# A decoder layer with a 32-expert mixture: the first expert's rows turned from an early gather and one-hot products, and the gathers and loads reordered around them

## Chip, cores and metric

One core of one Trainium2 chip. The metric is the device time of one launch in microseconds (us), the median over runs. The granted TensorE clock stands in the profile as a share of full speed: 1.00 is 2.4 GHz, 0.50 is 1.2 GHz.

## The reference, cut to what matters

```python
x  = x + merged @ w_out                      # (1024, 1024), the "x2" of the kernel
h2 = rms_norm(x, norm2_g)
# hier_moe: top-1 of 4 groups, then top-2 of its 8 SwiGLU experts
gl = h2 @ w_gr + b_gr;  g_idx = argmax(gl);  p_g = softmax(gl)[g_idx]
el_sel = (h2 @ w_er + b_er).reshape(N, 4, 8)[g_idx]
top_v, top_i = top_k(el_sel, 2)
w = softmax(top_v) * p_g
out[token] += w * (silu(xb @ w_gate[e]) * (xb @ w_up[e])) @ w_down[e]    # 32 experts, blocks of 128 rows
```

All of it in float32. The 1024 tokens are eight tiles of 128, and each expert serves its tokens in one block of up to 128 rows.

## The kernel before, in words

The kernel is written engine by engine, with semaphores; each engine runs its own list in order. float32 products are made of three products of split operands (high times high, high times low, low times high; `split3`, L105 to L107), so every weight piece is copied to a rounded "high" by ScalarE (`w_high`, L1186) and its remainder "low" is subtracted by VectorE (`w_low`, L1747).

**Output projection and routing.** `out_proj(cnt, ...)` runs 16 units, eight tiles for each half of the columns; VectorE adds the residual (`add_residual`, L1673) into `x2`. In the second eight units the router follows each tile: TensorE turns half a tile (`turn_half`, L838), ScalarE copies it out (`turned_half`, L1168), TensorE makes 36 logits (`route_half`, L851), VectorE finds group and experts (`top_group`, `two_experts`), TensorE counts earlier tokens of each expert (`positions_of`, L862 and L864), VectorE makes one-hot rows of the slot (`place_rows`, L1738 to L1741), and `rows_of` (L871) accumulates a table of token numbers: after eight tiles column e of `ids_rows` holds expert e's tokens. SyncE stores each finished tile of `x2` to `x2_dram` and to the output.

**Experts.** One round for each expert. POOL gathers its rows from `x2_dram` with an indirect DMA (`gather_rows`) into `xe[j % 4]`, TensorE turns them (`turn_x`, L571; for the first expert L956), ScalarE scales them by the norm's gain (`xs`, L1194) and makes `xeH`, VectorE makes `xeL`, and TensorE runs gate and up (`gate_up`, four pieces) and down (`down`, two pieces of the expert before). The result is added to rows gathered again from the output and scattered back (POOL).

**Weight loads.** Each expert has six pieces of 1 MB. SyncE issues all 192 in order of use (`load_piece(q)`) into ten slots; from q = 10 on each waits until the piece ten before it has been used (`w_used`). Pieces 0 to 3 are the first expert's gate and up, 4 to 7 the second's, 8 and 9 the first's down pieces. Pieces 0 and 1 are issued after the first eight projection units, 2 after the fourth store of `x2`, 3 after the last projection unit. Pieces 4 and later wait for the first gather (`xe_landed0`), and 8 waits for all stores of `x2`.

## Time and profile before

| what | value |
|---|---|
| median of 3 runs (lowest, highest) | 1482.78 us (1482.42, 1483.3) |
| the profiled execution's own time | 1481.47 us |
| its span | 1479.7 us |
| busy: PE, PEld, DVE, ACT, POOL | 96%, 81%, 68%, 56%, 28% |
| loads and other traffic on q1 | 263.79 MB of 286.39 MB |

PE is TensorE's matmul side and PEld its weight load, DVE VectorE, ACT ScalarE, POOL GpSimd, SP SyncE (SPq its queue). A `[... <-X]` at the end of a timeline row is idle time before it and what ended it. "DMA share" is the mean busy share of the core's 16 DMA engines. A matmul's duration holds its latency; the distance from start to start is what it costs in a stream.

### The profile page before, as it was taken

What the parts mean: (1) busy time and instruction counts of PE and PEld (TensorE: products, weight loads), DVE (VectorE), ACT (ScalarE), POOL (GpSimd) and SP (SyncE); (2) the same over time, 40 slices, a digit from 0 to 9 for tenths busy, and PEclk for the clock granted to TensorE, in tenths of its full rate; (3) what the DMA queues carried; (4) which work ended last, traced back from release to release, by engine and by line L of the source; (5) the groups of instructions that cost most, each with busy time, mean ns of one, the idle gap of its engine ahead of it and who ended that gap; (6) DMA issues with size and microseconds to landing.
All of it is one profiled execution on the core that took longest, in us unless ns stands there. A gap on an engine that the chain in (4) does not pass through costs nothing.

```text
span 1479.7 us, 19519 instructions
## 1 busy us (share of the span) xinstructions
PE 1424.3 (96%) x7296; PEld 1199.5 (81%) x7297; DVE 1008.1 (68%) x1444; ACT 828.9 (56%) x1342; POOL 407.7 (28%) x462
## 2 busy tenths in 40 slices
PE   5899999999999999999999979999999999999996
PEld 5788888888888788888888867888888888888885
DVE  6855664664574533344332567999999999999996
ACT  5653453353353322233232227888888888888883
POOL 3225424424433400000000011233333333333331
PEclk9999999999999999999999988999999999999999
DMA  7010110210210143354330549999999999999992
GB/s 220 23 44 12 51 44 1 62 43 1 61 44 0 44 115 99 86 149 121 91 142 36 198 152 385 375 386 385 392 386 387 386 389 389 393 396 393 389 384 89
DMA packets 134032, 286.39 MB, mean 194 GB/s; under 512 B 18864, under 2 KB 97840, under 8 KB 109360
## 3 DMA queue, kind: packets, MB, share of 16 engines
q1 hardware_dynamic: 119216, 263.79, 49.3%
q0 software_dynamic: 13248, 21.00, 3.8%
q8 instruction: 60, 0.98, 0.3%
q10 hardware_dynamic: 1472, 0.32, 0.1%
q14 instruction: 36, 0.29, 0.1%
HBM read 287.16 MB, written 25.17 MB: 211 GB/s over the span
## 4 chain that ended last, share of the span: by engine, by line
PE 85%; DMA 4%; DVE 4%; ACT 2%; POOL 2%; issue 2%; POOLq 0%; DVEq 0%; ACTq 0%
PE proj L105 17%; PE proj L107 16%; PE proj L106 16%; PE scores L105 6%; PE scores L107 6%; PE scores L106 6%; DMA w_slot<-in_w_up 4%; PE outs L760 2%; PE scores L693 2%; PE scores L571 1%; PE turned L105 1%; PE turned L107 1%; PE turned L106 1%; PE outs L851 1%; DVE w_low L1747 1%
## 5 line engine op out<-in xcount | busy, mean ns | idle before, releaser
L1747 DVE TENSOR_TENSOR w_low<-w_slot,w_high 128x2048 fp32r<-128x2048 f32 x192 | 430.9, 2285 | 0.1
L1186 ACT ACTIVATE w_high<-w_slot 128x2048 fp32r<-128x2048 f32 x190 | 352.6, 1907 | 20.1 <-DMA w_slot<-in_w_up 8.5
L105 PE MATMUL proj<-w_high,xeH 128*128 128x512 f32 x512 | 203.8, 398 | 3.9 <-DVE xeL L1850 1.9
L107 PE MATMUL proj<-w_high,xeL 128*128 128x512 f32 x512 | 200.6, 392 | 0.0
L106 PE MATMUL proj<-w_low,xeH 128*128 128x512 f32 x512 | 200.1, 391 | 0.0
L1376 POOL DMA_INDIRECT out<-y,ids_rows x31 | 86.5, 2791 | 342.8 <-DVE y L1860 342.8
L999 ACT ACTIVATE wCH<-wC_in 128x1024 fp32r<-128x1024 f32 x48 | 47.6, 1052 | 154.1 <-DMA wC_in<-in_w_branch_b 154.1
L1442 DVE TENSOR_TENSOR wCL<-wC_in,wCH 128x1024 fp32r<-128x1024 f32 x48 | 56.9, 1237 | 92.3 <-ACT wCH L999 92.3
L105 PEld LDWEIGHTS proj<-w_high,xeH 128*128 128x128 f32 x512 | 97.0, 189 | 25.5 <-issue 3.7
L107 PEld LDWEIGHTS proj<-w_high,xeL 128*128 128x128 f32 x512 | 96.5, 188 | 20.9
L106 PEld LDWEIGHTS proj<-w_low,xeH 128*128 128x128 f32 x512 | 96.7, 189 | 19.2
L105 PE MATMUL proj<-wBH,hTH 128*128 128x512 f32 x256 | 111.5, 435 | 0.0
L105 PE MATMUL proj<-wAH,hTH 128*128 128x384 f32 x256 | 99.1, 387 | 5.2 <-DVE wAL L1437 3.7
L107 PE MATMUL proj<-wBH,hTL 128*128 128x512 f32 x256 | 101.0, 395 | 0.0
L106 PE MATMUL proj<-wBL,hTH 128*128 128x512 f32 x256 | 100.3, 392 | 0.0
L105 PE MATMUL scores<-w_high,hidH 128*128 128x512 f32 x248 | 99.6, 402 | 0.0
L107 PE MATMUL scores<-w_high,hidL 128*128 128x512 f32 x248 | 96.9, 391 | 0.0
L106 PE MATMUL scores<-w_low,hidH 128*128 128x512 f32 x248 | 96.6, 390 | 0.0
L107 PE MATMUL proj<-wAH,hTL 128*128 128x384 f32 x256 | 87.7, 343 | 0.0
L106 PE MATMUL proj<-wAL,hTH 128*128 128x384 f32 x256 | 87.5, 342 | 0.0
L1194 ACT ACTIVATE xs<-scores,small 128x128 f32<-128x128 f32 x256 | 69.8, 385 | 5.1 <-PE scores L571 5.1
L1364 POOL DMA_INDIRECT xe<-x_rows,ids_rows x32 | 59.6, 1864 | 36.5 <-DVE ids_rows L1770 21.2
(299 smaller groups left out, 3167.4 us busy)
## 6 DMA issues: line engine op xcount, KB each, us to landing
w_slot<-in_w_gate SPq DMA_DIRECT2D x64, 1024.0 KB, 11.1
w_slot<-in_w_up SPq DMA_DIRECT2D x64, 1024.0 KB, 11.2
w_slot<-in_w_down SPq DMA_DIRECT2D x64, 1024.0 KB, 11.7
wC_in<-in_w_in SPq DMA_DIRECT2D x32, 512.0 KB, 4.8
wB_in<-in_w_in SPq DMA_DIRECT2D x16, 512.0 KB, 6.1
wA_in<-in_w_in SPq DMA_DIRECT2D x12, 512.0 KB, 5.9
x_all<-in_x SPq DMA_DIRECT2D x4, 1024.0 KB, 8.8
wC_in<-in_w_branch_a SPq DMA_DIRECT2D x16, 256.0 KB, 5.7
```

The costliest lines, as they stand in the source:

```text
L105: pe.matmul(out, lh, rh, start=start, stop=False)
L106: pe.matmul(out, lh, rl, start=False, stop=False)
L107: return pe.matmul(out, ll, rh, start=False, stop=stop)
L693: pe.matmul(SC[:, c, t0 * 128:t1 * 128], q_part[r, 0, :], k_part[r, 1 + t0:1 + t1, :].rearrange("p a b -> p (a b)"), start=q_part is qkTH ...
L760: last = pe.matmul(OB[:, 0:128], aT[:, j, :], V[:, j, :], start=(j == 0), stop=(j == i2))
L999: act.activation(wCH[sub][:, piece * 8:piece * 8 + 8, :], wC_in[sub][:, piece * 8:piece * 8 + 8, :], ACT.Copy).then_inc(S["wC_high"], 1)
L1186: act.activation(w_high[slot][:], w_in6[slot][:], ACT.Copy).then_inc(S["w_split"], 1)
L1194: act.activation(xs[:, k, :], SC[:, 0, k * 128:(k + 1) * 128], ACT.Copy, scale=g2x[:, k:k + 1]).then_inc(S["xs_done"], 1)
L1364: pool.indirect_dma_start(out=xe[j % 4][:], out_offset=None, in_=x2_dram, in_offset=ids_of(ids_rows, j), bounds_check=1023, oob_is_err=Fal ...
L1376: pool.indirect_dma_start(out=out_rows, out_offset=ids_of(ids_rows, j), in_=rows[:], in_offset=None, bounds_check=1023, oob_is_err=False). ...
L1442: dve.tensor_tensor(wCL[sub][:, r, :], wC_in[sub][:, r, :], wCH[sub][:, r, :].bitcast(F32), ALU.subtract).then_inc(S["wC_low"], 1)
L1747: dve.tensor_tensor(w_low[slot][:], w_in6[slot][:], w_high[slot][:].bitcast(F32), ALU.subtract).then_inc(S["w_lows"], 1)
```

## The change

1. Six tiles' table. `positions_of(5)` moves ahead of `route_half(14)` in unit 15, and `rows_of(4)` and `rows_of(5)` into unit 15; VectorE places tile 5 first and writes `first_ids`, the first expert's tokens of tiles 0 to 5. POOL gathers these rows into `xe[1]` at once, while tiles 6 and 7 are still being routed.
2. Tiles 6 and 7 go to the first expert by products: `x2` of each is split into `x2_high` (ScalarE) and `x2_low` (POOL), and `first_late` multiplies both with the one-hot matrix `first_pick` (VectorE) and accumulates onto the turned rows of the early gather, in two banks. The sum of squares of these rows is put together in the same way (`late_ss`, `first_r`).
3. `rows_of(6)`, `rows_of(7)` and the full table follow behind the first expert's first piece; then POOL gathers the second expert's rows first, and the first expert's (needed for the result) after them.
4. Pieces 4, 5 and 6 are loaded without a wait; piece 7, the eighth, waits until the second expert's rows have landed, and all later pieces stand behind it in SyncE's list.
5. The router's chain is two VectorE steps shorter for each tile (logits in two scaled additions of which one runs early, group mask in one). The low part of piece 2 is made in VectorE's iteration 4, and its high in ScalarE's unit 11, where both came after the units before.
6. VectorE scales the first expert's turned rows by the gain (`first_scaled`), where ScalarE did; the low part of its first half is made k by k.

```diff
-R_DIFFS, R_WEIGHTS = 90, 107
+R_DIFFS, R_WEIGHTS = 85, 102
...
+N_EARLY = 6
...
             for i in range(4, N_TILES - 1):
                 store_x2(i)
             sp.wait_ge(S["d_done"], 16)
             load_piece(3)
             store_x2(N_TILES - 1)
-            sp.wait_ge(S["xe_landed0"], DMA)
             for q in range(4, 6 * N_EXP):
+                if q == 7:
+                    sp.wait_ge(S["xe_landed1"], 2 * DMA)
                 if q == 8:
-                    sp.wait_ge(S["x2_stored"], N_TILES * DMA)
-                    sp.wait_ge(S["out_stored"], N_TILES * DMA)
+                    sp.wait_ge(S["x0_T"], 2)
+                    sp.wait_ge(S["early_stored"], 2 * N_EARLY * DMA)
+                    sp.wait_ge(S["late_stored"], 2 * (N_TILES - N_EARLY) * DMA)
                 load_piece(q)
...
+                if cnt == 15:
+                    positions_of(5)
                 if cnt >= 1:
                     route_half(cnt - 1)
...
+                if cnt == 15:
+                    rows_of(4)
+                    rows_of(5)
                 out_proj(cnt, range(5, 8))
...
+            def first_early():
+
+                pe.wait_ge(S["xe_landed1"], DMA)
+                for k in range(8):
+                    pe.matmul(first_turned(k), xe[1][:, DS(k, 128, step=8)], ident, start=(k % 4 == 0), stop=False, is_transpose=True)
+
+            def first_late(t, ks):
+
+                pe.wait_ge(S["place_step"], FIRST_HOT[t])
+                pe.wait_ge(S["x2_lows"], t - N_EARLY + 1)
+                for k in ks:
+                    for part in (x2_high, x2_low):
+                        last = pe.matmul(first_turned(k), part[t - N_EARLY][:, DS(k, 128, step=8)], first_pick[t - N_EARLY][:, :],
+                                         start=False, stop=(t == 7 and k % 4 == 3 and part is x2_low))
+                return last
+
             turn_half(15)
+            positions_of(6)
             route_half(15)
-            positions_of(6)
-            rows_of(5)
+            first_early()
+            first_late(6, range(4))
             positions_of(7)
-            rows_of(6)
-            rows_of(7)
...
+            first_late(6, range(4, 8))
+            first_late(7, range(4)).then_inc(S["x0_T"], 1)
+            first_late(7, range(4, 8)).then_inc(S["x0_T"], 1)
...
-                if cnt in (9, 10):
+                if cnt in (9, 10, 11):
                     high(w_high[cnt - 9][:], w_in6[cnt - 9][:], S[f"w_land{cnt - 9}"], DMA, S["w_split"])
...
+            for i in range(2):
+                act.activation(x2_high[i][:], x2[:, N_EARLY + i, :], ACT.Copy).then_inc(S["x2_highs"], 1)
+            act.wait_ge(S["xe_landed1"], DMA)
+            act.activation(first_sq[:], xe[1][:], ACT.Square, scale=1.0 / 32, accum_out=first_ms[:]).then_inc(S["first_sum"], 1)
+            act.wait_ge(S["xs_done"], 4)
+            for k in range(4):
+                act.activation(xeH[:, k, :], xs[:, k, :], ACT.Copy).then_inc(S["x0_H"], 1)
+            act.wait_ge(S["xs_done"], 8)
+            act.wait_ge(S["route_step"], R_DIFFS)
+            act.activation(xeH[:, 4:8, :], xs[:, 4:8, :], ACT.Copy).then_inc(S["xeH_done"], 1)
             high_piece(3)
...
+                if i == N_EARLY + 1:
+                    pool.wait_ge(S["xe_zero"], 1)
+                    pool.wait_ge(S["early_stored"], 2 * N_EARLY * DMA)
+                    pool.wait_ge(S["tables_done"], 1)
+                    pool.indirect_dma_start(out=xe[1][:], out_offset=None, in_=x2_dram[0:N_EARLY * 128, :],
...
+            for i in range(2):
+                pool.wait_ge(S["x2_highs"], i + 1)
+                pool.tensor_tensor(x2_low[i][:], x2[:, N_EARLY + i, :], x2_high[i][:].bitcast(F32), ALU.subtract).then_inc(S["x2_lows"], 1)
...
+            pool.wait_ge(S["x0_T"], 2)
+            pool.wait_ge(S["first_sum"], 1)
+            gather_rows(1)
             gather_rows(0)
-            gather_rows(1)
...
+            first_scaled(0)
+            for k in range(4):
+                dve.wait_ge(S["x0_H"], k + 1)
+                dve.tensor_tensor(xeL[:, k, :], xs[:, k, :], xeH[:, k, :].bitcast(F32), ALU.subtract).then_inc(S["x0_L"], 1)
+            dve.wait_ge(S["x0_T"], 3)
+            dve.wait_ge(S["first_sum"], 1)
+            dve.tensor_tensor(first_r[:], OB[:, 0:1], first_ms[:], ALU.add).then_inc(S["first_norm"], 1)
+            for t in range(N_EARLY, N_TILES):
+                pick_rows(t)
+            first_scaled(1)
...
+            dve.wait_ge(S["xeH_done"], 1)
+            dve.tensor_tensor(xeL[:, 4:8, :], xs[:, 4:8, :], xeH[:, 4:8, :].bitcast(F32), ALU.subtract).then_inc(S["xeL_done"], 1)
+            dve.wait_ge(S["rows_mm"], 8)
+            dve.tensor_tensor(ids_rows[:, 0:32], bank(3)[:, 32:64], w_rows[:, 0:32], ALU.add).then_inc(S["tables_done"], 1)
```

TensorE's list behind the last projection unit, before (`keyid` is the numbered token table, `xe` the gathered rows):

```order
L851 MATMUL outs<-wr,x2T 128x36 x3
L862 MATMUL scores<-mask,count_masks 128x32 [waits before_done,place_step]
L864 MATMUL scores<-before,count_masks 128x32
L871 MATMUL scores<-keyid_154,picks 128x32 [waits place_step]
L871 MATMUL scores<-keyid_154,picks 128x32
L862 MATMUL scores<-mask,count_masks 128x32 [waits before_done,place_step]
L864 MATMUL scores<-before,count_masks 128x32
```

and the same place in the changed kernel:

```order
L868 MATMUL outs<-wr,x2T 128x36 x3
L923 MATMUL turned<-consts,xe_221 128x128 [waits xe_landed1]
L923 MATMUL turned<-consts,xe_221 128x128 x3
L923 MATMUL proj<-consts,xe_221 128x128 x4
L931 MATMUL turned<-first_pick_167,x_high_231 128x128 [waits x2_lows,place_step]
L931 MATMUL turned<-first_pick_167,x_low_233 128x128
L931 MATMUL turned<-first_pick_167,x_high_231 128x128
L931 MATMUL turned<-first_pick_167,x_low_233 128x128
L931 MATMUL turned<-first_pick_167,x_high_231 128x128
L931 MATMUL turned<-first_pick_167,x_low_233 128x128
L931 MATMUL turned<-first_pick_167,x_high_231 128x128
L931 MATMUL turned<-first_pick_167,x_low_233 128x128
```

Behind these stand `positions_of(7)` and 24 more rows of L931. The turning of the gathered rows and the first eight products of tile 6 now stand ahead of the counting of tile 7.

POOL's list, before:

```order
L1351 TENSOR_TENSOR rstd_132<-ms_131,consts 128x1 [waits n2_rstd]
L1355 MEMSET xe_216 128x1024 [waits lg_done]
L1364 DMA xe_216<-x_rows,ids_rows 128x1024 [waits tables_done,x2_stored,xe_zero]
L1364 DMA xe_217<-x_rows,ids_rows 128x1024
```

and changed (`x_low` is `x2_low`; `xe_221` is `xe[1]`):

```order
L1412 DMA xe_221<-x_rows,first_ids 128x1024 [waits tables_done,early_stored,xe_zero]
L1416 TENSOR_TENSOR ms_131<-ms_131,ssq 128x1 [waits n2_sq]
L1418 TENSOR_TENSOR rstd_132<-ms_131,consts 128x1 [waits n2_rstd]
L1422 TENSOR_TENSOR late_ss<-ssq 128x1 x2
L1426 TENSOR_TENSOR x_low_233<-x_123,x_high_231 128x1024 [waits x2_highs]
L1426 TENSOR_TENSOR x_low_234<-x_123,x_high_232 128x1024 [waits x2_highs]
L1428 MEMSET xe_220 128x1024 [waits lg_done]
L1430 TENSOR_SCALAR first_r<-first_r 128x1 [waits first_norm]
L1432 TENSOR_TENSOR first_r<-first_r,consts 128x1 [waits first_norm]
L1441 DMA xe_221<-x_rows,ids_rows 128x1024 [waits x0_T,tables_done,first_sum,late_stored,xe_zero]
L1441 DMA xe_220<-x_rows,ids_rows 128x1024
```

POOL has two products of 1024 columns between the early gather and the second expert's.

SyncE's list, before:

```order
L527 DMA w_slot_190<-in_w_gate 128x2048 [waits xe_landed0]
L527 DMA w_slot_191<-in_w_up 128x2048
L527 DMA w_slot_192<-in_w_gate 128x2048
L527 DMA w_slot_193<-in_w_up 128x2048
L527 DMA w_slot_194<-in_w_down 128x2048 [waits out_stored,x2_stored]
```

and changed:

```order
L540 DMA w_slot_194<-in_w_gate 128x2048
L540 DMA w_slot_195<-in_w_up 128x2048
L540 DMA w_slot_196<-in_w_gate 128x2048
L540 DMA w_slot_197<-in_w_up 128x2048 [waits xe_landed1]
L540 DMA w_slot_198<-in_w_down 128x2048 [waits late_stored,early_stored,x0_T]
L540 DMA w_slot_199<-in_w_down 128x2048
L540 DMA w_slot_190<-in_w_gate 128x2048 [waits w_used]
```

The names' numbers differ by four between the two kernels: the first row of each is piece 4. The wait has moved from piece 4 to piece 7.

## Rows read from the trace of the kernel before

**Rows 1.** Windows: us, busy us of the engines, granted clock, DMA share, GB/s.
```profile
884.00:892.00 8.00, 2.04 (x9) 1.67 (x9) 2.37 (x2) 4.29 (x13) 3.06 (x4) 0.50 0.50 151
892.00:910.00 18.00, 17.79 (x92) 15.25 (x92) 13.09 (x21) 9.42 (x15) 0.00 (x0) 0.90 1.01 405
950.00:1000.00 50.00, 50.00 (x239) 41.96 (x238) 47.42 (x28) 42.73 (x50) 17.09 (x8) 1.00 1.00 381
1400.00:1440.00 40.00, 39.51 (x189) 32.75 (x188) 36.92 (x22) 33.41 (x36) 13.14 (x6) 1.00 1.01 385
```

**Rows 2.** The chain that ended last, expert rounds: start us, us, what.
```profile
1319.00 0.47 PE turned L571 x4
...
1336.77 0.47 PE turned L571 x4
...
1384.19 17.92 DMA w_slot<-in_w_up
...
1421.07 17.67 DMA w_slot<-in_w_up
```

**Rows 3.** Loads issued at 888.01, 889.34, 1055.67, 1375.59; us to landing at the end.
```profile
w_slot<-in_w_gate SPq DMA_DIRECT2D x1, 1024.0 KB, 7.5
...
w_slot<-in_w_up SPq DMA_DIRECT2D x1, 1024.0 KB, 13.7
...
w_slot<-in_w_down SPq DMA_DIRECT2D x1, 1024.0 KB, 6.8
...
w_slot<-in_w_down SPq DMA_DIRECT2D x1, 1024.0 KB, 18.6
```

**Rows 4.** Load issued at 844.94; us to landing.
```profile
w_slot<-in_w_gate SPq DMA_DIRECT2D x1, 1024.0 KB, 7.3
```

**Rows 5.** Timeline, a late projection unit: start us, us, what.
```profile
852.68 0.60 ACT L1168 ACTIVATE x2T<-scores 128x512 f32<-128x512 f32 x1 [0.53 <-PE scores L838]
...
854.55 0.97 PE L851 MATMUL outs<-wr,x2T 128*128 128x36 f32 x8
...
874.56 1.90 ACT L1186 ACTIVATE w_high<-w_slot 128x2048 fp32r<-128x2048 f32 x1
```

**Rows 6.** Timeline between the last projection and the first expert product.
```profile
872.62 0.69 DVE L1673 TENSOR_TENSOR x<-proj,x 128x512 f32<-128x512 f32 x1 [0.75 <-PE proj L107]
...
876.25 0.20 DVE L1706 TENSOR_TENSOR logits<-outs,logits 128x36 f32<-128x36 f32 x1 [0.62 <-PE outs L851]
...
879.23 0.22 DVE L1732 TENSOR_TENSOR keyid<-sorted,consts_late 128x64 fp32r<-128x64 f32 x1
...
882.06 0.19 DVE L1770 TENSOR_SCALAR ids_rows<-scores 128x32 int32<-128x32 f32 x1 [0.77 <-PE scores L871]
...
883.27 1.32 POOL L1364 DMA_INDIRECT xe<-x_rows,ids_rows  x1 [6.12 <-issue]
...
888.04 1.97 PE L956 MATMUL scores<-consts,xe 128*128 128x128 f32 x8 [5.88 <-DMA xe<-x_rows,ids_rows]
...
891.93 0.77 PE L105 MATMUL proj<-w_high,xeH 128*128 128x512 f32 x1 [1.92 <-DVE xeL L1850]
```

**Rows 7.** Gathers on POOL's queue issued at 883.27 and at 910 to 912; us to landing.
```profile
xe<-x_rows,ids_rows POOLq DMA_INDIRECT x1, 4.7
...
xe<-x_rows,ids_rows POOLq DMA_INDIRECT x1, 8.7
```

**Rows 8.** Groups by form, VectorE: mean ns of one.
```profile
L1741 DVE TENSOR_TENSOR picks<-consts_late,pos 128x256 fp32r<-128x256 f32 x8 | 3.4, 425 | 0.3
...
L1850 DVE TENSOR_TENSOR xeL<-xs,xeH 128x512 fp32r<-128x512 f32 x2 | 1.4, 693 | 6.4 <-ACT xeH L1228 6.4
```

**Rows 9.** Groups by form, POOL.
```profile
L1320 POOL TENSOR_TENSOR gatedR<-onR,sg 128x128 f32<-128x128 f32 x32 | 25.9, 810 | 2.5
...
L1343 POOL TENSOR_TENSOR wr<-wr,g_cols 128x288 f32<-128x288 f32 x1 | 1.0, 1042 | 132.7 <-DMA small<-in_norm_g 132.7
...
L1349 POOL TENSOR_TENSOR ms<-ms,ssq 128x1 f32<-128x1 f32 x8 | 1.5, 190 | 51.0 <-ACT x_sq L1161 51.0
```

More of the change, by code:

```diff
@@ L38 @@
 N_GROUPS = 4
+NO_SLOT = 4096.0
+N_EARLY = 6
+PLACED = {t: 2 * t + 2 + max(t - N_EARLY + 1, 0) for t in range(N_TILES)}
+FIRST_HOT = {t: PLACED[t] - 2 for t in range(N_EARLY, N_TILES)}
 def expert_at(j):
@@ L269, in decoder_layer @@
         gtop = rt("gtop", [P, 1])
-        gneg = rt("gneg", [P, 4])
+        far = rt("far", [P, 2])
+        late_ss = rt("late_ss", [P, 2])
+        first_ids = rt("first_ids", [P, 1], I32)
         el = rt("el", [P, 4, 8])
@@ L305, in decoder_layer @@
         r_rows = rs("r_rows", [P, 256])
+        first_pick = [sb(f"first_pick{i}", [P, 128], F32R, at=R_WORK + 16 * KIB + (i + 1) * KIB + 512) for i in range(2)]
         rc = region(merged_at[1] + 16 * KIB, merged_at[1] + 16 * KIB + 1152)
@@ L951, in last_down @@
                     last.then_inc(S["w_used"], 1)
-            pe.wait_ge(S["xe_landed0"], DMA)
-            for half, done in ((0, "x0_T"), (1, "xeT_done")):
-                for k in range(4 * half, 4 * half + 4):
-                    last = pe.transpose(SC[:, 0, k * 128:(k + 1) * 128], xe[0][:, DS(k, 128, step=8)], ident)
-                last.then_inc(S[done], 1)
             for e in range(N_EXP):
@@ L1865, in last_rows @@
                 dve.wait_ge(S[f"again_landed{e % 2}"], DMA * ((e - N_GROUPS) // 2 + 1))
-                for half, done in ((0, "y_half"), (1, "y_out")):
+                for half in range(2):
                     cols = slice(half * 512, half * 512 + 512)
```

178 lines of the change are left out of this document (105 added, 73 removed).

## The prediction

> **What bounds the kernel now.** I read the windows first, then the chain of waits, the loads' times to landing, and the timeline around the first expert. TensorE is busy without a gap in nearly every window, so at first sight it is the bound, and the hole between the last projection unit and the first expert looks like pure gain: between 872.6 and 891.93 little of it runs, at half clock in 884 to 892 [rows 1, 6]. The change goes at that hole.
>
> But the loads have no slack. From 892 on the 16 DMA engines are at a share of 1.00 to 1.01 with 381 to 405 GB/s, and it is no different in 1400:1440, with 385 GB/s [rows 1]. The time from a load's issue to its landing tells how much is queued: 6.8 us at 1055.67, 18.6 us at 1375.59 [rows 3]. Until then TensorE sets the round, 17.77 us from turn to turn (1319.00, 1336.77). Afterwards the chain runs through a load, and two rounds take 36.88 us (1384.19 to 1421.07), 18.44 each [rows 2]. **So the end is set by the stream of loads**, by when it starts in earnest (888.01, piece 4) and how much it has to bring. TensorE's lead is worth only what the queue can take up.
>
> **Before the gap.** ScalarE now makes piece 2's high in unit 11. The load is issued at 844.94 and lands 7.3 us later, at 852.2 [rows 4]; the high takes 1.90 (row at 874.56), to 854.1. Unit 12's square and copy, which now begin at 851.4 and 852.68, follow; the copy ends at 855.4, and route_half, which starts at 854.55, waits for it: **+0.85 us** [rows 5]. In unit 15 two table pairs move ahead of the last products; at some 0.15 us each in the stream, with a wait of 0.25 for tile 5's one-hot rows (0.425 long [rows 8]), I take **+0.5**. The last residual moves from 872.62 to 874.0 [rows 6].
>
> **The early gather.** first_ids is ready behind four or five VectorE steps of 0.2 us after route_half(14), at about 872.9. Before, the table (882.06, 0.19 long) was followed by the gather at 883.27, 1.0 us later [rows 6]; so the gather is issued at 873.9. It lands 4.7 us later on idle DMA engines and 8.7 under a full queue [rows 7]: at 878.6 or 882.6. Piece 3, two stores and pieces 4 to 6, about 5 MB in all, are issued within 2 us of it, so I take a value nearer the loaded row, 7.1, and 881.0. The Trainium skill (DMA: Bandwidth & Descriptors, Queues, rings and completion order) says that a DMA engine takes turns between its queues a packet at a time, which would put the gather near the unloaded row; the second rival is what follows then.
>
> **The turned rows.** TensorE stands in order: eight turns, 1.97 us at half clock (888.04 [rows 6]); eight products of tile 6, by the same price 1.7; the counting of tile 7, 0.4; then sixteen products. The clock came back about 4 us after products began (half in 884:892, 0.90 over 892:910 [rows 1]), so I take those at full speed, 0.11 each: 1.8 us. The first half is complete at T = 881.0 + 2.0 + 1.7 + 0.4 + 1.8 = **886.9**. Two other chains end earlier. Tile 7's experts: the logits step moves from 876.25 to about 877.9, and what stands up to 879.23 loses two steps: ready at 880.7 [rows 6]. POOL's remainders: the highs end at 877.3, then two subtractions of 1024 columns. No such row exists; less the 0.19 of a one-column step, 288 columns take 0.85 us and 128 take 0.62 [rows 9], so 3.2 or 5.2 us each, and I take 3.2, nearer in size: both at 883.7, before TensorE reaches them at 886. The Trainium skill (GPSIMD Engine Reference, Elementwise — side-by-side cycle accounting) counts 2.6 cycles an element, an estimate of 2.2 us; by it the sum stays and the third rival loses.
>
> **From T to the second expert's rows.** VectorE: scale 0.7 (0.69 for 512 columns [rows 8]); four highs and lows by turns, to T + 2.4; first_r and two one-hot pairs 1.0; second scale 0.7; two router steps 0.4; ScalarE's high of the second half 0.7, its low 0.7, the table 0.2: T + 6.1. TensorE's first product stands at T + 1.5 and its table pairs behind twelve products, T + 4.7 to 6.5, hidden either way. Then 1.0 to the gather and 4.7 to land, the DMA engines being idle by then (the 5 MB are through at about 886.5): T + 11.8 = **898.7**. All that time SyncE stands at piece 7, with every later piece behind it, although the slots are free.
>
> **What that is worth.** Before, piece 7 landed at 889.34 + 13.7 = 903.0; the first load after the restart lands 7.5 later, as at 888.01 [rows 3], so at 906.2: the stream is **3.2 us behind**. Break-even would be rows landed at 895.5. TensorE itself is ahead: 888.4 against 891.93, and some 3.0 at the second expert, since VectorE's weights and lows still stand there. It then has 6.2 us more queued in front of it than before. The little air that the queue had (381 GB/s in 950:1000 against 385 when the loads set the pace [rows 1]; 1% of 70 us, and a queue of 6.8 us that was not always full on each engine) gives back 0.7 to 2; I take 1.2. Sum: **+2.0 us**. The turned copies, the shorter router steps and the tail cost or bring nothing beside that: the first stand beside loads or in the chains above, the tail is the same. The profiled execution took 1481.47, so 1483.5; the median is 1.3 above it, so **1484.8**. 0.2%, about what a measurement can tell here, is 3.0 us: the forecast is within it. Bounds of this case: gather at 878.6 and 2 given back, -1.2; gather at 882.6, half clock for all products (+1.8) and nothing given back, +6.6.
>
> **Rivals.**
> - *The loads catch up* (faster). The time to landing falls from 13.7 us to 6.8 in the early rounds [rows 3]; if the queue has that much air, all 6.2 us are drained before it fills again, and TensorE's lead counts: 3.0, or 5.4 with the gather at 878.6. That gives 1477.4 to 1479.8. It decides once 6 us are given back where I count 1.2. Against it stands the share of 1.00 in just those rounds. 0.22.
> - *The gather is served at once.* Landing at 878.6, T is 884.5, the second rows land at 896.3, +0.8 and 1.2 given back: 1482.4, nothing to be measured. The change then does what it says, the first product comes 6 us earlier, and the loads hide it. 0.20.
> - *POOL's remainders are last* (slower). At 5.2 us each the second is ready at 887.7, T is 888.6, the rows land at 900.4: +4.9 and 1.2 given back, 1486.5. It decides above 4.3 us a subtraction. 0.10.
> - *Forecast*: loads set the end and restart about 3 us later. 0.48, of which 0.14 ends above 1485.8.
>
> **How the numbers follow.** Faster than 1479.8: 0.18 of the first rival and 0.02 of the second. Slower than 1485.7: 0.10 and 0.14. The rest, 0.56, is within 0.2%. The range takes in most of the first rival and the forecast up to +4.6: 1478.6 to 1487.4.
>
> **What would show it.** Right: the early gather's landing near 881, first product near 888, the second expert's rows and piece 7's issue near 899, a hole in DMA activity before it, times to landing that reach 18 us some rounds earlier than 1375 and rounds of 18.4 from there. Each term is wrong if its time is off by more than 1.5 us. The whole reading is wrong if rounds stay at 17.77 to the end or begin to stretch no earlier, for then the queue had air, and TensorE's lead is the gain.

## The result, and the profile after

The changed kernel takes 1487.47 us (median of 7, 1486.64 to 1490.17) against 1483.3 for the kernel before on the same chip (7 runs, 1481.12 to 1483.61): ratio 1.003, 95% interval 1.002 to 1.004. It is **slower by 4.2 us**, just above the range, where the forecast said no change that can be measured. The profiled executions have spans of 1485.6 and 1479.7; about 1.0 of that difference stands before anything that the change touches (the first weight load is issued at 816.55 after, at 815.58 before). Single executions of 1604.76 us (the kernel before), 3031.7 us (b_hold_before) and 3671.91 us (c_early46) were in a slower state and are in none of the medians and ratios below.

The windows answer to [rows 1]: us, busy us of PE, PEld, DVE, ACT, POOL, granted clock, DMA share, GB/s.

```profile
884.00:892.00 8.00, 8.00 (x36) 8.00 (x35) 1.72 (x6) 0.58 (x3) 0.00 (x0) 0.50 0.70 293
892.00:910.00 18.00, 18.00 (x91) 15.61 (x92) 14.19 (x33) 11.17 (x20) 4.75 (x4) 0.86 0.28 89
...
1400.00:1440.00 40.00, 39.49 (x182) 31.95 (x182) 37.09 (x22) 33.69 (x36) 16.12 (x7) 1.00 0.97 380
```

TensorE's hole is filled: 8.00 of 8 us busy in 884 to 892, where it was 2.04. What took its place is in the DMA columns: 18 us at a share of 0.28 and 89 GB/s, where before it was 1.01 and 405. The hole moved from TensorE to the DMA engines that bring the weights.

The chain of waits that ended last, between the early gather and the second gather's table and later on (answers to [rows 2]):

```profile
872.74 0.17 DVE first_ids L1839
...
873.91 8.60 DMA xe<-x_rows,first_ids
...
882.56 1.12 PE turned L923 x4
...
884.53 1.79 PE turned L931 x8
...
886.66 1.97 PE proj L931 x8
888.64 1.92 PE turned L931 x8
890.56 1.92 PE proj L931 x8
...
897.89 0.36 PE scores L893 x4
898.28 0.19 DVE ids_rows L1885
...
1249.89 0.47 PE turned L586 x4
...
1261.33 17.93 DMA w_slot<-in_w_up
...
1389.72 17.88 DMA w_slot<-in_w_up
...
1426.59 17.99 DMA w_slot<-in_w_up
```

Every link from the early landing to the table is TensorE's, and half of that time goes to 32 products at 0.24 us each, where 0.11 or 0.21 had been counted. Rounds are 17.77 us up to 1249.89, and a load stands in the chain from 1261.33. Before, the first load in this part of the chain stands between 1336.77 and 1384.19, where [rows 2] leave lines out:

```profile
1348.21 17.01 DMA w_slot<-in_w_up
```

So the loads enter the chain 87 us, some five rounds, earlier than before. That is the sign that the prediction gave for a late stream.

Timeline of the same stretch (answers to [rows 6]):

```profile
877.15 4.65 POOL L1426 TENSOR_TENSOR x_low<-x,x_high 128x1024 fp32r<-128x1024 f32 x2 [0.38 <-ACT x_high L1275]
...
877.66 1.89 DVE L1778 SCALAR_TENSOR_TENSOR logits<-logits,rstd,br 128x36 f32<-128x36 f32 x1
879.59 0.26 DVE L1780 SCALAR_TENSOR_TENSOR logits<-outs,rstd,logits 128x36 f32<-128x36 f32 x1
...
880.07 1.75 DVE L1785 SCALAR_TENSOR_TENSOR gsc<-logits,gmax,consts_late 128x4 f32<-128x4 f32 x1
...
890.69 0.69 DVE L1844 TENSOR_TENSOR xs<-turned,small 128x512 f32<-128x512 f32 x1 [3.06 <-PE turned L931]
...
893.09 0.77 PE L109 MATMUL proj<-w_high,xeH 128*128 128x512 f32 x1
...
898.28 0.19 DVE L1885 TENSOR_TENSOR ids_rows<-scores,w_rows 128x32 int32<-128x32 f32 x1 [1.76 <-PE scores L893]
...
899.40 2.84 POOL L1441 DMA_INDIRECT xe<-x_rows,ids_rows  x1 [4.88 <-ACT silu_ready L1287]
```

The first expert product stands at 893.09; before, it was at 891.93 [rows 6]. The change's own aim, an earlier first expert, is not met: 0.2 us later once the 1.0 of the execution is taken off. Time to landing of the early gather (issued at 873.91), of the second expert's (899.40), and of the loads issued at 905.62 and 908.97 (answers to [rows 3, 7]):

```profile
xe<-x_rows,first_ids POOLq DMA_INDIRECT x1, 8.6
...
xe<-x_rows,ids_rows POOLq DMA_INDIRECT x1, 6.2
...
w_slot<-in_w_up SPq DMA_DIRECT2D x1, 1024.0 KB, 5.3
...
w_slot<-in_w_up SPq DMA_DIRECT2D x1, 1024.0 KB, 19.1
```

Piece 7 is issued at 905.62 and landed at 910.9, against 903.0 before: 7.9 us late, or 6.9 with the execution's 1.0 taken off.

### The profile page after: what moved, and what is told of

Same layout as the page of the kernel before. It is cut to its first block, busy times and chain, and to the rows that moved or that the text cites. A ratio compares the mean times of both kernels' runs of the same rounds, so it can differ in the third digit from the quotient of the medians.

```text
span 1485.6 us, 19603 instructions
## 1 busy us (share of the span) xinstructions
PE 1434.3 (97%) x7332; PEld 1207.5 (81%) x7333; DVE 1011.8 (68%) x1448; ACT 829.6 (56%) x1339; POOL 416.1 (28%) x468
## 4 chain that ended last, share of the span: by engine, by line
PE 81%; DMA 7%; DVE 5%; issue 2%; ACT 2%; POOL 2%; SPq 0%; POOLq 0%; ACTq 0%; DVEq 0%
PE proj L109 16%; PE proj L111 15%; PE proj L110 15%; DMA w_slot<-in_w_up 6%; PE scores L109 6%; PE scores L111 6%; PE scores L110 6%; PE outs L777 2%; PE scores L710 2%; DVE w_low L1836 2%; PE scores L586 1%; PE turned L109 1%; PE turned L111 1%; PE turned L110 1%; PE outs L868 1%
```

## Experiments

Four calls, each on one chip with its own runs of the kernel before (medians 1482.5, 1483.2, 1483.0 and 1483.1); all ratios are against these, five rounds each. Times of the trace are from each kernel's profiled execution, whose first loads are issued up to 1.4 us apart; "start taken off" means that this difference to the kernel before has been subtracted.

### First call: the hold, the stream, the gather

**a_nohold**, the changed kernel without the hold:

```
             for q in range(4, 6 * N_EXP):
-                if q == 7:
-                    sp.wait_ge(S["xe_landed1"], 2 * DMA)
                 if q == 8:
```

> The changed kernel without the wait of the eighth piece for the second expert's rows; pieces 8 and later still wait for the first expert's turned rows. Theory (the stream of loads sets the end, and the hold restarts it at 905.6 instead of about 896): piece 7 goes out at 878, pieces 8 and later at about 892, the stream is some 13 us ahead of the changed kernel's; the rounds stay at 17.77 us to the end, and the time is set by TensorE: about 1481 to 1483 us, 4 to 6 us below the changed kernel. The second expert's rows are then gathered under load and land 8 to 9 us after issue instead of 6.2, about 908; TensorE then waits about 2 us for them, which is in that range. Rival (the hold is harmless, the end moved because TensorE's own path got longer): 1487 us or more, since the gather now lands later.

Measured: 1485.35, ratio 1.0019 (1.0011 to 1.0028). The expectation was too low. Rounds stay at 17.77 until 1392, and a load stands in the chain only from 1386.26, later even than before the change. Taking the hold out brings less than expected: the loss against the kernel before falls from 4.2 to 2.9 us in the medians (the two intervals overlap) and from 4.9 to 1.7 in the profiled executions, start taken off. What remains is TensorE's: the second gather now takes 8.3 us to land beside the loads, and the second expert's first product stands at 912.95 (before: 910.47), 2.1 later with the start taken off.

**b_hold_before**, the kernel before with only a late stream:

```
             for q in range(4, 6 * N_EXP):
+                if q == 7:
+                    sp.wait_ge(S["w_used"], 4)
```

> The kernel before with one wait more: piece 7, and with it all later pieces, waits until the first expert's fourth piece has been used (about 905). TensorE's, VectorE's, ScalarE's and POOL's work is unchanged. Theory: the stream restarts about as late as in the changed kernel, pieces 4 to 6 having landed; loads come to bind around 1250, rounds of 18.4 us from there, and the time rises by 4 to 6 us to about 1487 to 1489. Rival (loads are prefetched ten deep and catch up, the change's loss has another cause): within 1 us of the kernel before.

Measured: 1488.74, ratio 1.0039 (1.0025 to 1.0052), as the theory said. Piece 7 at 905.77, the first product at 892.12 as ever. Its chain from the early rounds to the end:

```profile
1225.82 0.88 PE scores L573 x8
...
1243.60 0.88 PE scores L573 x8
...
1261.40 17.86 DMA w_slot<-in_w_up
```

This is the changed kernel's picture to 0.1 us (1261.33), made with one wait. A restart at 905.8 alone costs about 6 us. The changed kernel's loss is 4.2 with the same restart; its interval overlaps with this one's. Its pieces 4 to 6 land 10 us sooner (890.8 against 900.8 for piece 6), but no run shows that this is the difference.

**c_early46**, the kernel before with pieces 4 to 6 let go at once, as the change does:

```
-            sp.wait_ge(S["xe_landed0"], DMA)
             for q in range(4, 6 * N_EXP):
+                if q == 7:
+                    sp.wait_ge(S["xe_landed0"], DMA)
```

> The kernel before with pieces 4, 5 and 6 issued at once behind piece 3 (about 874) and piece 7 waiting for the first gather. Theory: the first gather lands 1 to 4 us later, at 889 to 892, because the engines still carry the early pieces, but the stream is 5 to 7 us ahead; the rounds stay at 17.77 us to the end and give back the 2.2 us that the loads took in the last four rounds. Sum between -1.2 and +2 us: 1482 to 1485 us, with no stretched rounds. Rival (the gather is served at once): -2 us, 1481. Rival (loads do not bind): plus the gather's delay, 1484 to 1487.

Measured: 1486.53, ratio 1.0026 (1.0015 to 1.0036). The theory was too low; the time lies where the second rival put it, in which loads don't bind and the gather's delay counts. The first gather (issued 884.23) takes 7.6 us instead of 4.7 beside the early pieces, and the first product stands at 895.78. The stream is ahead (piece 7 lands at 897.4 instead of 903.0), and yet TensorE's lateness, 3.5 us at the second expert with the start taken off, comes out at the end in full (3.7 in the profiled executions). So bytes that run ahead were paid for in the gather's landing, and in the kernel before it is TensorE's path that counts, not the start of the stream.

**d_46_later**, the changed kernel with pieces 4 to 6 behind the early landing:

```
             store_x2(N_TILES - 1)
+            sp.wait_ge(S["xe_landed1"], DMA)
             for q in range(4, 6 * N_EXP):
```

> The changed kernel with pieces 4, 5 and 6 behind the landing of the early gather; the hold of piece 7 stays. Theory: the early gather, issued at 873.9 beside piece 3 and two stores only, lands 6 to 7 us after issue instead of 8.6, the first turned half, the table and the second expert's rows all come 2 us earlier, the stream restarts at about 903.5, and the time falls by 1 to 2 us to 1485.5 to 1486.5. Rival (the gather's landing does not depend on the loads beside it): no change, 1487.5.

Measured: 1487.63, ratio 1.0031 (1.0019 to 1.0043), as the rival said. The early gather still takes 8.8 us. It is not these three pieces that it waits behind.

### Second call: how late is late, and the products

**f_hold2_before**: as b_hold_before with `w_used` at 2 in place of 4.

> The kernel before with piece 7 held until the first expert's second piece is multiplied: the hold that ran with the fourth piece, shorter. Piece 7 then starts near 899 instead of 888, about where the prediction put the restart of the stream (898.7), and lands near 907. This asks whether the step from the lateness of the stream to the end was right. Theory (about half or more of any lateness is kept to the end once it is over a few us): restart at 899 gives +2.5 to +4, so 1485 to 1486.5. Rival (the prediction's step: 1.2 us of it is given back, and the rest counts, against 903.0 for the landing before): +2.0, and if slack takes it all up, 1482.5 to 1483.

Measured: 1483.01, ratio 1.000 (0.9991 to 1.0009). Piece 7 at 899.48, and it costs **nothing** that can be measured (within 1.3 us either way): the theory falls, and of the rival only its edge holds. The loads show why (landing, us):

| load | before | restart 899.5 | restart 905.8 | changed |
|---|---|---|---|---|
| piece 7 | 903.0 | 904.9 | 910.9 | 910.9 |
| piece 13 | 918.9 | 921.5 | 928.1 | 928.1 |
| piece 31 | 971.0 | 971.3 | 978.9 | 979.0 |
| piece 79 | 1114.5 | 1113.8 | 1120.9 | 1121.2 |
| piece 151 | 1335.1 | 1335.1 | 1341.1 | 1340.9 |

Landings are the issue plus the time to landing. 2.6 us of lateness are gone within three rounds; 9.2 shrink to 8 by then and to 6 at the end. Before, a load of these rounds took 6.8 us (issued at 1055.67 [rows 3]) and was issued when its slot came free, so a small delay is caught up there. The changed kernel's loads are all queued longer there; the one issued at 1054.42 takes:

```profile
w_slot<-in_w_up SPq DMA_DIRECT2D x1, 1024.0 KB, 13.0
```

**h_no_low**, the changed kernel without the low parts of tiles 6 and 7 (their 16 products and two subtractions are left out):

```
-                    for part in (x2_high, x2_low):
+                    for part in (x2_high,):
```

> The changed kernel without the low parts of tiles 6 and 7: 16 of the 32 products and both subtractions are left out (so the first expert's rows from these two tiles are rounded). This takes 16 x 0.24 = 3.9 us out of the stretch between the early landing and the second gather. Theory (the products at half clock stand in full before the first product and before the restart of the stream): first product near 889.3, piece 7 near 901.8 instead of 905.6, and 2 to 3.5 us off the end: 1484 to 1485.5. Rival (the two landings of the gathers set the restart and slack takes the rest): within 1 us of the changed kernel.

Measured: 1485.51, ratio 1.0016 (1.0007 to 1.0025). First product 889.44, piece 7 at 902.35, second expert's first product 909.07: 3.2 to 3.7 us earlier in each place, so up to there the products stand in the path in full. The median is 2 us lower than the changed kernel's, but the intervals overlap, and the profiled execution (1487.36 us, among the slower ones of its kernel) doesn't show the gain at its end. It loses the lead at once: the third expert's first product stands at 929.21, against 929.96 in the changed kernel, because in front of it ScalarE waits 1.68 and 1.82 us for loads, against 0.32 and 1.67. With a restart at 902.35, what TensorE wins is taken back by the loads.

**g_low_dve**, the changed kernel with the subtractions on VectorE:

```
-                pool.tensor_tensor(x2_low[i][:], x2[:, N_EARLY + i, :], x2_high[i][:].bitcast(F32), ALU.subtract).then_inc(S["x2_lows"], 1)
...
+            low_rows(0)
             top_group(7)
             two_experts(7)
+            low_rows(1)
```

> The changed kernel with nothing but the two subtractions of the low parts moved from POOL to VectorE. Theory (VectorE's two operations of 1.89 and 1.75 us are the price of POOL's subtractions, not of the operations): both are back at 0.2 to 0.3 us, tile 7's chain is ready near 882 even with 2.2 us of subtractions on VectorE, and the time stays within 0.5 us of the changed kernel's (1487) since the gather's landing at 882.5 and the order on TensorE come last. Rival (they are slow through something else, such as the DMAs' traffic): they stay over 1.5 us.

Measured: 1487.92, ratio 1.0035 (1.0021 to 1.0049). The timeline of VectorE:

```profile
877.41 1.23 DVE L1846 TENSOR_TENSOR x_low<-x,x_high 128x1024 fp32r<-128x1024 f32 x1
878.56 0.25 DVE L1775 SCALAR_TENSOR_TENSOR logits<-logits,rstd,br 128x36 f32<-128x36 f32 x1
...
879.32 0.22 DVE L1782 SCALAR_TENSOR_TENSOR gsc<-logits,gmax,consts_late 128x4 f32<-128x4 f32 x1
...
881.52 0.15 DVE L1808 TENSOR_SCALAR far<-mask 128x1 f32<-128x1 f32 x1
```

1.89 and 1.75 us are back at 0.25 and 0.22, and tile 7's chain ends at 881.7 instead of 883.95 although VectorE also made the first subtraction by then. In the changed kernel the second slow operation ends at 881.82, and POOL's two subtractions at 877.15 + 4.65 = 881.80. The kernel's time does not move, since the count of tile 7 stands behind the early turns on TensorE.

**e_products_first** puts what the runs so far showed together, on a_nohold: the low parts on VectorE; tile 6's products and tile 7's count before the gather lands; the early rows turned into banks of their own and scaled while tile 7's products run; one-hot rows and row products of tiles 6 and 7 ahead of the first piece; the gather for the second expert ahead of first_r. The core of it on TensorE and VectorE:

```
-            first_early()
-            first_late(6, range(4))
+            first_late(6, range(8))
             positions_of(7)
-            first_late(6, range(4, 8))
-            first_late(7, range(4)).then_inc(S["x0_T"], 1)
...
+            first_early()
+            rows_of(6)
+            first_late(7, range(4)).then_inc(S["x0_T"], 1)
+            first_late(7, range(4, 8)).then_inc(S["x0_T"], 1)
+            rows_of(7)
...
+                for k in range(4 * half, 4 * half + 4):
+                    dve.scalar_tensor_tensor(xs[:, k, :], bank(6 - half)[:, k % 4 * 128:k % 4 * 128 + 128], g2x[:, k:k + 1], xs[:, k, :],
+                                             ALU.mult, ALU.add).then_inc(S["xs_done"], 1)
```

> The changed kernel without the hold on piece 7, rearranged so that nothing of tiles 6 and 7 stands between the early gather and the first product that need not: low parts subtracted on VectorE (2 x 1.1 us) and not on POOL, the 16 products of tile 6 made before the gather lands and the count of tile 7 too, the turned rows in banks of their own and scaled while the products of tile 7 run, picks and row products of tiles 6 and 7 ahead of the first piece. Theory (the late first product and the held stream are two separate prices, and both are paid by where the work stands, not by the gather itself): landing at 882.5, turns 2.0, 16 products 3.9 at half clock, first gate product near 889.5 instead of 893.1 (before 891.9), second expert's gather issued near 891 instead of 899, pieces 8 and 9 near 889; loads at least as early as before's everywhere, so 1479.5 to 1481.5, 1 to 3 us below before. Rival (loads bound the end whatever the products do, and early bytes are given back): 1482 to 1483, same as before.

Measured: **1480.44** (9 runs, before 1483.23), ratio 0.9977 (0.9967 to 0.9987). It is faster than both kernels. Its timeline and windows:

```profile
883.20 1.12 PE L922 MATMUL scores<-consts,xe 128*128 128x128 f32 x4
...
889.50 0.78 PE L109 MATMUL proj<-w_high,xeH 128*128 128x512 f32 x1
```

```profile
890.81 1.06 POOL L1434 DMA_INDIRECT xe<-x_rows,ids_rows  x1 [12.33 <-DVE ids_rows L1888]
```

```profile
894.00:898.00 4.00, 4.00 (x22) 3.39 (x21) 3.23 (x8) 3.99 (x4) 0.86 (x2) 1.00 1.02 407
898.00:902.00 4.00, 4.00 (x20) 3.30 (x19) 3.59 (x13) 1.11 (x1) 0.00 (x0) 1.00 0.95 377
```

First product at 889.50, as expected; second gather at 890.81 instead of 899.40; no hole in the DMA columns; second expert at 908.61 against 910.47. So an early gather can pay: what cost time was the order around it. Several things changed at once here, and no run tells what each of them is worth.

### Third call: hold, piece 3, clock

**i_products_first_hold**: e_products_first with the hold on piece 7 put back.

> The rearranged kernel (products first, 1480.4) with nothing but the hold on piece 7 behind the second gather put back. The gather is now issued at 890.8 instead of 899.4, so with the hold it lands near 895.5 and piece 7 goes there, 8 us later than before's 888 but 10 earlier than the changed kernel's 905.6. Theory (lateness of the stream is free up to a restart near 899 and costs about 0.9 us for each us beyond it): the hold costs nothing now, 1480 to 1481.5. Rival (the hold's 2 us is a price of its own, whenever the gather goes): 1482 to 1483.

Measured: 1480.71, ratio 0.9986 (0.9977 to 0.9996). Piece 7 at 894.99; the interval overlaps with that of the kernel without the hold, as the theory said. In the profiled executions both are 2.6 us ahead of the kernel before at about 1230, and the one with the hold gives back 1.2 us more of that by the end. So the hold has no fixed price of 2 us; one of about 1 us can't be excluded.

**j_piece3_late**, the changed kernel with piece 3 behind the early landing:

```
-            load_piece(3)
             store_x2(N_TILES - 1)
+            sp.wait_ge(S["xe_landed1"], DMA)
+            load_piece(3)
```

> The changed kernel with piece 3 behind the early gather's landing as well (its store of tile 7 stays ahead). Before issued its first gather with nothing beside it but the end of pieces and it landed in 4.7 us; the early gather landed in 8.6 beside piece 3 and the stores, and holding pieces 4 to 6 alone did not change that. Theory (piece 3's megabyte is what the gather waits behind): landing at 878.7 to 880, first product 1 to 3 us earlier in the trace; but pieces 3 to 6 start 3 to 5 us later, and the tile 7 products wait for POOL and VectorE, so the time is 1485.5 to 1487.5. Rival (the stores, or the gather's reading of rows just written, make it long): landing stays at 882 or later and the time is 1487 to 1489.

Measured: 1486.69, ratio 1.0025 (1.0015 to 1.0035). The early gather's landing (issued 872.99):

```profile
xe<-x_rows,first_ids POOLq DMA_INDIRECT x1, 5.6
```

5.6 us instead of 8.6 to 8.8, beside the two stores alone, as the theory said: with pieces 4 to 6 held too, piece 3's megabyte is worth 3 us. First product 890.03, piece 7 at 902.43.

**l_busy_changed**, the changed kernel with 43 added products whose results nobody reads, and **k_busy_first**, the same idea on e_products_first with 34:

```
+            keep_busy(7, 5)
             turn_half(15)
+            keep_busy(6, 5)
             positions_of(6)
             route_half(15)
+            keep_busy(30, 5)
             first_early()
```

> The changed kernel with 43 added products of 256 columns, whose results nobody reads, in TensorE's waits up to the early gather's landing. It tests the step of the prediction that took the 32 late products at full clock. Theory: the clock stays at full, turns take 1.0 and the 32 products about 4 instead of 7.8, the first product comes near 888.5 (the prediction's 888.4) instead of 893.1, piece 7 near 901 instead of 905.6, and the time is 1483 to 1485.5. Rival: half clock all the same, the added products last till 885 and push all that follows by 2 to 3 us: 1488 to 1490.

Measured: 1487.99, ratio 1.0034 (1.0023 to 1.0046). Windows and timeline:

```profile
882.00:884.00 2.00, 1.50 (x11) 1.51 (x11) 1.48 (x10) 1.15 (x2) 0.44 (x1) 1.00 1.02 430
884.00:886.00 2.00, 2.00 (x11) 2.00 (x11) 0.19 (x1) 0.00 (x0) 0.00 (x0) 1.00 1.02 430
886.00:888.00 2.00, 2.00 (x10) 2.00 (x10) 0.60 (x3) 0.00 (x0) 0.00 (x0) 0.67 1.02 430
```

```profile
884.40 0.40 PE L931 MATMUL turned<-first_pick,x_high 128*128 128x128 f32 x1
884.64 0.41 PE L931 MATMUL turned<-first_pick,x_low 128*128 128x128 f32 x1
```

Neither theory. The clock is at full up to 886, the turns are quicker (0.9 us for eight from start to start instead of 1.6), and yet the products come every 0.24 us, as at half clock. The clock was never their price.

> The rearranged kernel (1480.4) with 34 added products of 256 columns, whose results nobody reads, in TensorE's waits between the last projection unit and the turns of the early rows. Theory (the clock falls to half near 877 because TensorE waits between 873.8 and 876.3, and stays there because what follows is thin): it stays at full, the 32 products take 0.12 us each instead of 0.24, and the first gate product comes at 886 to 887.5 instead of 889.5, with its piece at full clock too: 2 to 5 us ahead at the second expert, of which the loads let through at most 2: 1478.5 to 1480.5. Rival (the clock falls anyway): the added products stand in the way at half clock, first product at 890 to 893, 1480.5 to 1483.

Measured: 1482.22, ratio 0.9989 (0.9979 to 1.0), in the rival's range. Full clock up to 882, 0.24 us a product there too; the 12 products added last push the turns from 883.20 to 885.60.

### Fourth call: the products' operand

**m_busy_apart** is l_busy_changed with the parts laid out so that a product's operand is 128 neighbouring columns:

```
-                        last = pe.matmul(first_turned(k), part[t - N_EARLY][:, DS(k, 128, step=8)], first_pick[t - N_EARLY][:, :],
+                        last = pe.matmul(first_turned(k), part[t - N_EARLY][:, k * 128:k * 128 + 128], first_pick[t - N_EARLY][:, :],
-                act.activation(x2_high[i][:], x2[:, N_EARLY + i, :], ACT.Copy)
+                act.activation(x2_high[i][:].rearrange("p (k c) -> p k c", k=8), x2[:, N_EARLY + i, :].rearrange("p (c k) -> p k c", k=8), ACT.Copy)
```

> The changed kernel with the 43 added products, and with the high and low parts of tiles 6 and 7 written with the columns of each of the eight groups side by side, so that a product's stationary operand is 128 neighbouring columns and no longer every eighth. Theory (the stride of the weight load sets 0.24 us, the clock does not): while the clock is full the products take 0.11 to 0.13 each and their loads under 0.2, first product near 890 to 891, piece 7 near 902.5, 1485.5 to 1487. Rival (the fp32r type or 128 columns as such set it): 0.24 as before, 1488.

Measured: 1488.17, ratio 1.0033 (1.002 to 1.0046). The theory holds for the products and not for the time.

```profile
884.53 0.28 PE L931 MATMUL turned<-first_pick,x_low 128*128 128x128 f32 x1
884.64 0.28 PE L931 MATMUL turned<-first_pick,x_high 128*128 128x128 f32 x1
...
889.79 0.41 PE L931 MATMUL proj<-first_pick,x_high 128*128 128x128 f32 x1
890.00 0.41 PE L931 MATMUL proj<-first_pick,x_low 128*128 128x128 f32 x1
```

0.11 us a product at full clock, 0.21 once the clock has fallen. The weight loads say the same, in l_busy_changed and here, both at full clock:

```profile
884.32 0.34 PEld L931 LDWEIGHTS turned<-first_pick,x_high 128*128 128x128 f32 x1
```

```profile
884.36 0.19 PEld L931 LDWEIGHTS turned<-first_pick,x_high 128*128 128x128 f32 x1
```

**The stride of the operand sets 0.24 us, at either clock.** The engines that make the parts read with that stride now and pay for it: two highs take 4.32 us instead of 1.99, two subtractions on POOL 6.06 instead of 4.74, and tile 7's chain ends at 886.6, some 2 us later, behind them. The first product still comes 1.1 us earlier than in l_busy_changed, start taken off (891.88 against 892.15). The lead is lost by the third expert, whose first product stands at 932.00 against 929.43, 1.7 us later with the start taken off; in front of it ScalarE waits 1.70 and 1.87 us for loads, against 0.27 and 1.50. The second wait:

```profile
924.95 1.92 ACT L1252 ACTIVATE w_high<-w_slot 128x2048 fp32r<-128x2048 f32 x1 [1.87 <-DMA w_slot<-in_w_up]
```

**n_first_apart** (e_products_first with parts apart) and **o_busy_apart** (with parts apart and 22 added products) carry the same edit.

> The rearranged kernel (products first, no hold, 1480.4) with the high and low parts written apart as well. The clock is at half there; a gate's product of 512 columns takes 0.43 and an early turn 0.23 for 128 columns at half clock. Theory: products 0.15 to 0.22 each instead of 0.24, first gate product 0.3 to 1 us earlier, 1479.5 to 1480.5, hardly to be told from the rearranged kernel. Rival (subtractions with a strided operand get slower on VectorE, over 1.5 us each, and push tile 7's chain): 1480.5 to 1481.5.

> The rearranged kernel with parts written apart and with 22 added products in TensorE's waits up to tile 6's products only (none between these and the early turns, where 12 of them cost 2.9 us in k_busy_first). Theory (clock full until the turns, product 0.12): turns start at the landing, 882.5, tile 7's products end near 886.5 to 887.5, first gate product 887 to 888, second expert 2 to 4 us ahead of the rearranged kernel's 908.6; the loads let through less than half: 1479 to 1480.5. Rival (the clock falls in the wait before the landing): first gate product at 889.5, 1480 to 1481.

Measured: 1482.24, ratio 0.9991 (0.9982 to 1.0), and 1482.05, ratio 0.9993 (0.9984 to 1.0001). At half clock a product takes 0.21, but each subtraction on VectorE takes 2.0 us instead of 1.2, the first product stands at 890.86 and 890.78 instead of 889.50, and in o_busy_apart the clock falls all the same, where TensorE waits 1.71 us for the subtraction. Both lie above both of their ranges, and their medians lose to that of e_products_first by some 2 us in the ratio to the kernel before; the intervals overlap a little.

## Why the prediction was wrong

**What bounds the kernel: half right.** The prediction said "the end is set by the stream of loads, by when it starts in earnest", and that TensorE's lead is worth only what the queue can take up. b_hold_before shows the first for a stream that starts late enough. For the kernel before it is wrong. The table sets each kernel against the kernel before, in us. The second column is when piece 7 is issued (before: 889.3), the third TensorE's turn of the round at about 1230 in the profiled execution (before: 1230.13, start taken off), the fourth the median.

| kernel | piece 7 | TensorE at 1230 | median |
|---|---|---|---|
| a_nohold | 877.7 | +2.1 | +2.9 |
| c_early46 | 891.9 | +3.5 | +4.0 |
| e_products_first | 878.1 | -2.6 | -2.8 |
| k_busy_first | 877.9 | 0.0 | -0.8 |
| i_products_first_hold | 895.0 | -2.6 | -2.3 |
| n_first_apart | 878.1 | -1.8 | -0.9 |
| o_busy_apart | 878.0 | -0.5 | -1.0 |
| f_hold2_before | 899.5 | -0.1 | -0.2 |
| h_no_low | 902.4 | +0.9 | +2.3 |
| j_piece3_late | 902.4 | -1.5 | +3.7 |
| l_busy_changed | 904.8 | +0.7 | +5.0 |
| changed | 905.6 | +1.0 | +4.2 |
| b_hold_before | 905.8 | +1.3 | +6.2 |
| d_46_later | 906.2 | +1.7 | +5.1 |

With piece 7 issued by 899.5, the time follows TensorE's lead or lateness to within 1 us, about what the medians can tell, though the DMA share is 1.00 to 1.01 from 1000 to 1375 in the kernel before. From 902.4 on the loads add 1.4 to 5.2 us. (g_low_dve and m_busy_apart, with 905.7 and 905.3, are not in the table: their TensorE has waited for loads in the third expert already, and is 3.9 and 4.0 us behind at 1230; their medians are 4.7 and 5.1 above.) In the changed kernel's profiled execution they add 3.9 of the 4.9 us that it ends later. The prediction also read [rows 2] as if loads stood in the chain only after 1336.77 and close to 1384; they stand there from 1348.21.

**Piece 2's high, +0.85: nothing.** Its load landed 6.4 us after its issue (845.92 to 852.32) instead of 7.3. The copy behind the high ends at 855.35, ahead of route_half at 855.52, which is before's 854.55 plus the execution's 0.97. That 0.97 is also why the early gather's issue, 873.91, is the forecast to the hundredth: two errors cancel.

**The early gather, 7.1 us to land: 8.6.** Landing at 882.5 instead of 881.0. The second rival (served at once, 4.7) falls; d_46_later and j_piece3_late place the wait behind piece 3. The rule of the Trainium skill that this rival rested on (DMA: Bandwidth & Descriptors, Queues, rings and completion order: a DMA engine takes turns between its queues) did not bring the gather near the unloaded row in any run with a load beside it (7.6 to 8.8).

**T = 886.9: 890.56.** This is the step that failed most. The turns (2.0), the first eight products (1.8 for 1.7) and the counting came as said. "I take those at full speed, 0.11 each: 1.8 us" took 3.9. It was wrong twice. The clock did stay at half (0.50 through 884 to 892), but l_busy_changed shows that full clock would not have helped; the 0.11 belongs to an operand of neighbouring columns (m_busy_apart). The bound "half clock for all products (+1.8)" was near in size, for another reason.

**T + 11.8 = 898.7: T + 15.1 = 905.6.** The table pairs, "hidden either way", are not. Behind T stand the second half's eight products (1.9), four small ones for the sum of squares (0.8) and twelve of 512 columns (4.6: 0.43 each at half clock and 0.23 for the last three). The pairs come at 897.73, where T + 6.5 was the latest that had been counted, and VectorE waits 1.76 us for them: +1.8. The second gather takes 6.2 us instead of 4.7: +1.5. With T's 3.7 that makes 6.9, the whole of 905.6 against 898.7.

**Worth of lateness, 1.2 us given back: wrong in shape.** The profile of before showed loads of 6.8 us in rounds that were paced by TensorE, and I counted the share of 1.01 as no air. f_hold2_before, restarted at 899.5, loses nothing, so the predicted restart, had it come, would have cost nothing either, and the break-even is at 899.5 or later, not 895.5. With 905.8 the kernel before pays 6 us; between the two it was not run. The total is nearer than its steps, by luck: the restart was 6.9 us later than forecast, but the first load behind it landed in 5.3 us instead of 7.5, 1.0 of the lateness is the execution's start, and more was given back than the 1.2. So 4.2 was measured for 2.0. The prediction's own bound, with a gather of 8.7, half clock for the products and nothing given back, was +6.6; its range ended at +4.6.

**POOL's remainders: the rival falls, and left a mark elsewhere.** A subtraction takes 2.3 us (4.65 for two), not 3.2; the estimate of 2.2 from the Trainium skill's figure (GPSIMD Engine Reference, Elementwise — side-by-side cycle accounting) was the better one. But while they ran, two of VectorE's operations took 1.89 and 1.75 us; g_low_dve gives them back.

**The loads catch up: falls at this restart.** TensorE had no lead to give: its second expert is 0.8 us behind before's, the execution's start taken off. What this rival said of TensorE's lead, that it counts, is right where the stream is not held: e_products_first has a lead of 2.6 us and gains 2.8.

What stays open: why the granted clock falls at about 883 in k_busy_first and 886 in l_busy_changed while TensorE shows no idle time there (it had waited 0.32 us before 878.77 and 1.63 us before 882.50), and why the early turns, whose rows are strided too, come every 0.11 us at full clock (eight in 0.91 in l_busy_changed); no run looked at which of their operands is loaded, or whether its type matters (`xe` is fp32, the parts are fp32r).

## What to carry to other kernels

Work that fills an engine's wait is not free if something else waits behind it: here it filled TensorE's hole, and the loads, held behind it, restarted 16 us later than before. Here a DMA share of 1.00 went with 10 us of slack in the loads; whether they set the end is seen by holding them a little, and by making the engine a little earlier. Before pricing a small product from another row, look at its operand's stride as well as its columns and the clock. When an early copy of data must be merged with late data, put the products that don't need the copy ahead of its landing, the copy in its own place, and the next copy's table ahead of the work that it unblocks: that order, with the hold gone, made the same idea 2.8 us faster than the kernel before instead of 4.2 slower.

## What the runs showed of the hardware

- A product of 128 columns whose stationary operand takes every eighth fp32 column costs 0.24 us at full and at half clock; with neighbouring columns 0.11 and 0.21. The weight load goes from 0.34 to 0.19 us at full clock. Reading such a layout, ScalarE's copy of 1024 columns takes 2.0 to 2.2 us instead of 1.0, VectorE's subtraction 2.0 instead of 1.2, POOL's 3.0 instead of 2.3 to 2.4. The Trainium skill (SBUF — State Buffer, Door 1: The DMA port swizzle) states that each access that crosses to another 16-byte line of SBUF pays; a step of 32 bytes does so every time, and these rows agree. The early turns, with the same step and 0.11 us each at full clock, do not fit in and stay open.
- VectorE operations of 4 to 36 columns with two operands in SBUF took 1.75 to 1.89 us beside POOL's subtractions, 0.22 to 0.25 without them. The Trainium skill (SBUF — State Buffer, SBUF: two separate sides) states that a VectorE operation with two inputs in SBUF and a GpSimd operation that reads SBUF lock one port pair, each for its whole instruction. The traces agree: the second slow one ends with POOL's second subtraction (881.8), and the row between them (L1780, one operand in PSUM) takes 0.26 us.
- One megabyte issued beside an indirect gather of 128 rows cost the gather 3 us of landing (8.6 and 8.8 against 5.6). Three more megabytes behind it changed nothing (8.6 with them, 8.8 without).
- A stretch of 11 us without a new load (888.9 to 899.5) was caught up within some three rounds of an expert each; one of 17 us (889.1 to 905.8) was not by the end.
